# A float32 transformer layer on one core: the down projection turned from feature-major to token-major

## The reference

```python
def rmsnorm(x, g):
    y = x * rsqrt(mean(x * x, axis=-1, keepdims=True) + EPS)
    return y * g

def swiglu_ffn(h, w_gu, w_down):
    g, u = split(h @ w_gu, 2, axis=-1)
    return (silu(g) * u) @ w_down

h = x + gla_mixer(rmsnorm(x, norm_mix_g), ...)
h = h + swiglu_ffn(rmsnorm(h, norm_ffn_g), w_gu, w_down)   # w_down: 2816 x 1024
out = rmsnorm(h, final_norm_g)
```

## Time and profile before

| | us |
|---|---|
| median of 3 runs (lowest, highest) | 2302.48 (2296.62, 2304.03) |
| the profiled execution, its own time | 2303.43 |
| its span, first to last instruction | 2301.7 |
| PE busy | 2182.6 (95%) |
| POOL, DVE, ACT busy | 1614.2, 1338.3, 829.6 |
| mean granted TensorE clock | 0.978 of full |

### The profile page before, as it was taken

One profiled execution on the slowest core, in us unless ns is written; L12 is line 12 of the kernel. 1 busy time (PEld: TensorE's weight loads), 2 busy tenths in 40 slices (PEclk: granted clock), 3 DMA queues, 4 the chain that ended last, 5 costly groups with the idle time before them and its releaser, 6 DMA issues.

```text
span 2301.7 us, 28014 instructions
## 1 busy us (share of the span) xinstructions
PE 2182.6 (95%) x10040; PEld 1808.1 (79%) x10040; DVE 1338.3 (58%) x1765; ACT 829.6 (36%) x1430; POOL 1614.2 (70%) x1300
## 2 busy tenths in 40 slices
PE   6999999899989999789999998999999999999975
PEld 5888788778877888578888886888888788888864
DVE  5345544554555443376666664757575756578756
ACT  3224333333343332343434342444444322222313
POOL 5555675566556665668888885988888877776744
PEclk8999999999999999989999999999999999999988
DMA  4322354335433656563434359444343777667761
GB/s 130 104 82 74 110 170 132 110 111 172 139 110 99 201 158 217 181 233 137 173 129 177 128 180 358 154 149 160 142 164 138 297 262 295 261 244 261 291 256 73
DMA packets 233929, 400.56 MB, mean 174 GB/s; under 512 B 16864, under 2 KB 176608, under 8 KB 224832
## 3 DMA queue, kind: packets, MB, share of 16 engines
q1 hardware_dynamic: 199488, 357.82, 44.0%
q10 hardware_dynamic: 34304, 40.97, 5.3%
HBM read 271.85 MB, written 126.88 MB: 173 GB/s over the span
## 4 chain that ended last, share of the span: by engine, by line
PE 82%; DVE 6%; ACT 4%; DMA 4%; POOL 2%; issue 1%; SPq 0%; ACTq 0%; DVEq 0%; POOLq 0%
PE ps L651 26%; PE ps L653 25%; PE ps L652 25%; PE ps L681 1%; PE ps L765 1%; DVE xs L1368 1%; ACT junk L974 1%; DMA xop<-x_stage 1%; DVE lc L1396 1%; POOL ring_lo L594 1%; DMA hop<-stage 1%; DMA raw<-in_gla_w_out 1%; DMA xs<-in_x 1%; PE ps L738 1%; PE ps L742 1%
## 5 line engine op out<-in xcount | busy, mean ns | idle before, releaser
L602 POOL TENSOR_TENSOR w_op<-w_raw,w_op 128x512 fp32r<-128x512 f32 x330 | 473.5, 1439 | 160.9 <-ACT w_op L964 157.3
L651 PE MATMUL ps<-x_op,w_op 128*128 128x512 f32 x1232 | 484.3, 393 | 20.4 <-issue 12.0
L652 PE MATMUL ps<-x_op,w_op 128*128 128x512 f32 x1232 | 482.8, 392 | 0.0
L653 PE MATMUL ps<-x_op,w_op 128*128 128x512 f32 x1232 | 482.4, 392 | 0.0
L591 POOL TENSOR_SCALAR ring_hi<-raw 128x512 fp32r<-128x512 f32 x256 | 178.7, 698 | 337.9 <-issue 167.6
L594 POOL TENSOR_TENSOR ring_lo<-raw,ring_hi 128x512 fp32r<-128x512 f32 x256 | 350.2, 1368 | 21.3
L964 ACT ACTIVATE w_op<-w_raw 128x512 fp32r<-128x512 f32 x330 | 206.4, 628 | 365.0 <-PE ps L653 171.7
L651 PEld LDWEIGHTS ps<-x_op,w_op 128*128 128x128 f32 x1232 | 233.4, 189 | 72.3 <-issue 23.8
L653 PEld LDWEIGHTS ps<-x_op,w_op 128*128 128x128 f32 x1232 | 233.4, 189 | 48.8
L652 PEld LDWEIGHTS ps<-x_op,w_op 128*128 128x128 f32 x1232 | 233.6, 190 | 48.4
L651 PE MATMUL ps<-hid,w_op 128*128 128x512 f32 x616 | 242.6, 394 | 16.6 <-DVE acc L1745 16.1
(11 more groups left out here) (185 smaller groups left out, 3938.8 us busy)
## 6 DMA issues: line engine op xcount, KB each, us to landing
hop<-stage SPq DMA_DIRECT2D x154, 512.0 KB, 2.8
hid<-hop SPq DMA_DIRECT2D x70, 1024.0 KB, 9.5
raw<-in_gla_w_in SPq DMA_DIRECT2D x192, 256.0 KB, 3.2
w_raw<-in_ffn_w_gu SPq DMA_DIRECT2D x176, 256.0 KB, 3.9
xop<-x_stage ACTq DMA_DIRECT2D x56, 512.0 KB, 3.6
x_op<-xop SPq DMA_DIRECT2D x56, 512.0 KB, 11.1
w_raw<-in_ffn_w_down SPq DMA_DIRECT2D x88, 256.0 KB, 4.5
raw<-in_gla_w_out SPq DMA_DIRECT2D x64, 256.0 KB, 3.1
```

The lines of the kernel that those rows point to most:

```text
L602: pool.tensor_tensor(shaped(q, w_op[i][:, 1, :]), source(q, i), shaped(q, w_op[i][:, 0, :]).bitcast(F32), ALU.subtract).then_inc(op_ready[ ...
L651: pe.matmul(out, l_hi, r_hi, start=first, stop=False, skip_group_check=more)
L652: pe.matmul(out, l_hi, r_lo, start=False, stop=False, skip_group_check=more)
L653: return pe.matmul(out, l_lo, r_hi, start=False, stop=last, skip_group_check=more)
```

## The change

Only the down projection and what follows it change.

- The operands of the matmul are exchanged: a 128-token block of `hid` is stationary, the weight operand moves over all 512 columns. A lane is now a block of 128 tokens (four in each quarter), and the result is token-major, as the residual and the output are. All transposes go (`turn_final`, `turn_tail`).
- A quad is now one pair with all columns; a slice has one or two quads, and both operand sets are held at once (`w_op` and `w_op2`, `w_t2b`, `w_t3b`).
- Slices 0 to 4 of each half go product by product in the order 0, 1, 4, 3, 2, 5, 6 over all four lanes, with two banks for each lane (`BANK_D`); all eight banks are used. The last slice goes lane by lane.
- `hid` has 7 slots, not 9: slot `i` is filled again when product `i` of all four lanes of the slice before is done.
- The residual is added on DVE, SBUF to SBUF, in slices 1 and 3 of each half (`add_ht`, 128 x 1024 each). Product 0, which goes into four quarters, is kept in `p1_sum` up to slice 3 (lanes 0 and 1) or 4 (lanes 2 and 3), then added to three quarters (`spread_p1`), and from there on added three times from the bank.
- The final norm works on `acc` in place: token block by token block in the last slice and (for the rest of half 0) in the first slice of half 1. SP's queue gets the stores of half 0, and the loads of `ht`.

```diff
-        hid = [... for n in range(9)]
+        hid = [sb(f"hid{n}", MIX + 8192 * n, [P, 2, 2, T], F32R) for n in range(7)]
+        BANK_D = (0, 1, 0, 1, 0, 1, 0)
+        IN_TURN, BY_BANK = (0, 1, 2, 3, 4, 5, 6), (0, 1, 4, 3, 2, 5, 6)
+        SUMMED_TO = (3, 3, 4, 4)
+        HT_PARTS = (1, 3)
+        HT_AT = {1: 0, 2: 1, 5: 2, 6: 3}
...
@@ sync @@
             def load_hid(n, i):
+                if n == 0:
+                    sp.wait_ge(prod[i // 2], U_QUADS)
+                else:
+                    sp.wait_ge(prod[i], slices[n]["lane0"])
...
                 if n == 0:
                     for m in range(7):
                         store_hid(end, m)
+                        if m in (2, 4):
+                            load_quad(slices[1]["quads"][m // 2 - 1])
+                    sp.dma_start(g_fin[:, :], ...).then_inc(fin_loaded, 16)
+                    for slot in range(4):
+                        sp.wait_ge(stage_stored[slot], 16 * ((7 * NP * NS - slot + 3) // 4))
...
@@ tensor @@
+            def lane_product(n, l, i):
+                pairs = slices[n]["pairs"]
+                lane_free(n, l, i)
+                tok = slice(l * P, (l + 1) * P)
+                for j in range(pairs):
+                    w = (w_op, w_op2)[j][i]
+                    ins = three(ps[:, lane_bank(n, l, i), :], hid[i][:, j, 0, tok], hid[i][:, j, 1, tok], w[:, 0, :],
+                                w[:, 1, :], j == 0 and i < 3, j == pairs - 1, i > 2)
+                ins.then_inc(prod[i], 1)
+            for n, part in enumerate(slices):
+                if part["part"] == LAST_SLICE:
+                    steps = [(l, i) for l in range(4) for i in IN_TURN]
                 else:
+                    steps = [(l, i) for i in BY_BANK for l in range(4)]
...
@@ scalar: op_split @@
-                if q > 0:
-                    act.wait_ge(prod[i], lanes_end[q - 1])
+                if second(q) and slice_of[q][0] == 0:
+                    if i > 0:
+                        act.wait_ge(prod[3 if i <= 2 else 4], U_QUADS)
+                elif q > 0:
+                    act.wait_ge(prod[i], lanes_before(q))
...
+                elif q == U_QUADS - 1:
+                    for at, (i, j) in enumerate(made_in(0)):
+                        op_split(U_QUADS + j, i)
+                        if at in (4, 8, 11):
+                            hidden_hi(pair, (4, 8, 11).index(at))
...
+                if before["part"] == LAST_SLICE:
+                    for j in range(3):
+                        for number in range(4):
+                            square_of(0, j, number)
+                            if number == 0 and j > 0:
+                                root_of(0, j - 1)
...
@@ vector: gather @@
+                if i == 0 and part > SUMMED_TO[l]:
+                    for out_half, th in ((0, 1), (1, 1), (1, 0)):
+                        dst = place(n, l, out_half, th)
+                        ins = dve.tensor_tensor(dst, dst, bank, ALU.add)
+                    ins.then_inc(p1_kept, 1)
+                    return
...
+                            elif B == 0:
+                                if (l, i) == (1, 2):
+                                    variance_fin(0, 0)
+                                elif (l, i) == (1, 3):
+                                    root_fin(0, 0)
+                                elif (l, i) == (1, 4):
+                                    scale_fin(0, 0, 0)
+                                elif (l, i) == (2, 0):
+                                    scale_fin(0, 1, 0)
...
```

More of the change, by code:

```diff
@@ L647, in _, with weigh @@
+            def weigh(j, out_half, squares):
+                pool.wait_ge(squared, SQUARES["fin", 1, j] + squares)
+                cols = slice(out_half * HALF, (out_half + 1) * HALF)
+                tile = acc[1][1][j]
+                pool.tensor_tensor(tile[:, cols], tile[:, cols], g_fin[:, cols], ALU.mult).then_inc(tail_weighed, 1)
+            for j in range(4):
+                weigh(j, 1, 1)
+                weigh(j, 0, 3)
         @block.tensor
@@ L1732, in _ @@
                 sum_3(pair)
-            def place(q, column, out_half, token_half):
-                return acc[d_quads[q - U_QUADS]["B"]][:, column + 4 * out_half, token_half, :]
-            def gather(q, lane, column, product, bank, dst, done, n):
-                dve.wait_ge(prod[product], lane + 1)
-                from_bank = ps[:, 3 * (lane % 2) + bank, :]
-                if n == 0 and d_quads[q - U_QUADS]["part"] == FIRST_SLICE:
-                    ins = dve.tensor_copy(dst, from_bank)
-                else:
-                    ins = dve.tensor_tensor(dst, dst, from_bank, ALU.add)
-                ins.then_inc(done, 1)
@@ L1763, in _, with place @@
-            summed = 0
-            for q in range(U_QUADS, QUADS):
-                d = d_quads[q - U_QUADS]
-                tile = final_tile(q)
-                final = q == QUADS - 1
-                ending = d["part"] == LAST_SLICE and not final
-                def between(i):
-                    if final:
-                        for number in TAIL_AFTER[i]:
-                            tail_add(number)
-                    if q == U_QUADS:
+            def place(n, l, out_half, th):
+                return acc[slices[n]["B"]][th][l][:, out_half * HALF:(out_half + 1) * HALF]
@@ L1784, in between @@
                             sum_4(pair)
                             hidden_lo(pair, 6)
-                    if tile is not None and i == 2:
-                        dve.wait_ge(ht_loaded[tile % 2], 16 * (tile // 2 + 1))
-                        dve.wait_ge(fin_turned, tile + 1)
-                        for half in range(2):
-                            part = ht[tile % 2][:, half * HALF:(half + 1) * HALF]
-                            dve.tensor_tensor(part, part, ps[:, 6 + half, :], ALU.add).then_inc(fin_added, 1)
```

627 lines of the change are left out of this document (310 added, 317 removed).

## The result

| | kernel before | changed kernel |
|---|---|---|
| median of 4 runs | 2302.55 us (2296.62 to 2304.03) | 2280.65 us (2280.23 to 2281.34) |
| ratio | | 0.9905, 95% interval 0.9892 to 0.9917 |
| span of the profiled execution | 2301.7 | 2278.5 |
| first matmul on `hid` starts | 1824.70 | 1826.37 |
| last one starts | 2275.74 | 2268.62 |

The account below looks back on a forecast made before the run. PE, busy 95% of the span, was taken as the bound: last matmul at 2243.4 plus tail 10.1 gave 2253.5; stalls of 4, 3, 4.5 and 1.5 gave span 2266.5, so median 2267 us, range 2254 to 2286.

Parts of the forecast that it names:

- Pace and count: Down projection on PE: still 1848 matmuls at 0.2266 us, 418.7 us in all, with no transposes.
- Tail: Behind the last matmul: only lane 3's last quarter and two last stores, 10.1 us (9 to 13).
- The `y_all` block: Eight `y_all` loads ahead of raw weights in SP's queue: removing them saves 13.07 us and 2.4 of slow clock.
- Place 1: Start of down: late gathers behind ACT's hidden pieces, and a late `hid` load for slice 1; 4 us (0 to 10).
- Place 2: Slice 3 of each half: residual adds and spreads make DVE late for slice 4; 1.5 us each (0 to 4).
- Place 3: Last slices: 0.3 us lost in each of eight lanes, about 2 in lane 2 of half 0; 4.5 us (2 to 9).
- Place 4: First slice of half 1: DVE's wait for lane 3's squares covered unless Newton steps eat the slack; 1.5 us (0 to 5).
- POOL: Each slice: 14 splits and 8 sums take 30 of 38.1 us, so POOL is not the bound; no loss forecast.
- The slow clock behind a wait: PE at 1.2 GHz for part of the time: 2.4 us counted in the kernel before, nothing for new gaps.
- Rival A: Whole stage: all stalls covered except 0.3 us in each of eight lanes, giving 2257 us; chance 0.13.
- rival B: DVE becomes the bound in places through slow SBUF-to-SBUF operations: 36 us of stalls, giving 2290 us; chance 0.18.
- Rival C: SP's in-order queue holds up loads: four places at 13.1 us each, giving 2320 us, slower than before; chance 0.04.

Follow-up runs that it names:

- the first edit: Changed kernel with ACT's hidden pieces of the last pair made two places earlier: 2278.36 us, ratio 0.9900.
- three edits: On the changed kernel, each alone: ACT's hidden pieces earlier, 2278.36 us; root ahead of square in half 0's last slice, 2279.78; residual tile 2 added behind product 6, 2282.86.
- the two that relieved POOL: On the changed kernel: raw weights loaded by quarter as freed (alone 2276.57 us), and POOL's two last sums moved directly ahead of product 5's splits (not run alone).
- five edits: Changed kernel with quarter loads, earlier ACT pieces, root ahead of square, POOL's last sums later, and residual tile 2 added behind product 6: 2265.16 us, ratio 0.9839.

## Why the prediction was right, and where it was off

The sign, the range and the mechanism held; the sum of the stalls was mis-sized. Span 2278.5 against 2266.5 forecast, step by step:

- **Pace and count: right.** 1848 matmuls at 0.2266, no change by exchanging operands, no transposes.
- **Start of the stage: 1.7 of the 12.0.** It began at 1826.37 instead of 1824.70, and between 1820.53 and 1825.56 in the experiments. This is scatter of the stages before.
- **Tail: right in sum, by two errors that cancel.** 10.1 forecast, 9.65 measured. Up to the last store it took 5.2 instead of 4.6, with two gathers and two squares behind the last matmul where I had one of each; from the store to the end 4.5 instead of 5.5. (By the earlier trace rows the time between landing and the end was 7.5 - 5.3 = 2.2 before, not 1.5.) Its first and last rows:

```profile
2268.80 1.27 DVE L1803 TENSOR_TENSOR acc<-acc,ps 128x512 f32<-128x512 f32 x2
...
2272.85 1.28 DVE L1394 SCALAR_TENSOR_TENSOR acc<-acc,rstd,g_fin 128x1024 f32<-128x1024 f32 x1
2274.03 0.34 ACTq L1333 DMA_DIRECT2D out<-acc  x1
```

- **The `y_all` block: right.** 13.07 + 2.4 forecast; the run with that edit alone gave 16.9 by the medians and 15.5 in its profile.
- **Place 1, 4 forecast, 5.2 found.** The first half was right in kind: ACT's piece came behind splits and DVE waited for it, but ahead of the very first gathers of slice 0, for ACT itself had waited 9.64 us for POOL's last sums. DVE's and ACT's timelines:

```profile
1836.62 1.84 DVE L1370 TENSOR_TENSOR stage<-s,stage 128x512 fp32r<-128x512 f32 x1 [6.11 <-ACT stage L983]
...
1840.05 2.47 DVE L1801 COPY p_sum<-ps 128x512 f32<-128x512 f32 x4
```

```profile
1834.19 0.63 ACT L983 ACTIVATE w_op<-w_raw 128x512 fp32r<-128x512 f32 x1 [9.64 <-POOL w_raw L640]
```

  The `hid` load behind it was covered in this profile. In four others it came out with this delay in place, 0.2 to 1.8 us (1.17 in the changed kernel run again, near 1864 as I had said) and in the five without the delay it was 1.5 to 2.1.
- **Place 2, 3 forecast, 8.4 found** (3.64 + 4.74). The place and the engine were right, and so, nearly, was DVE's work: ahead of the last gathers of slice 3 stand three residual adds and six spreads, 3 x 3.0 + 6 x 1.5 = 18.0 by my allowance, and they took 17.2 in half 0 (with a wait of 2.75 for the tile's load, which stood in SP's queue behind loads of `hid`) and 18.3 in half 1, with one add of 5.62. PE idled 1.83 and 2.93, where I had 2 for this allowance and took 1.5. The slow clock behind the two waits added 1.8 each, and this is most of what was missing. Both rows are of DVE in the changed kernel:

```profile
1964.15 1.98 DVE L1822 TENSOR_TENSOR acc<-acc,ht 128x1024 f32<-128x1024 f32 x1 [2.75 <-DMA ht<-hres]
...
2159.82 5.62 DVE L1822 TENSOR_TENSOR acc<-acc,ht 128x1024 f32<-128x1024 f32 x1
```

  The same sum, taken in the nine profiles that have the adds in this order, tells whether there is a gap: up to 15.3 us there was none (seven places), from 15.5 to 18.4 PE idled the sum minus 15.35 (ten places, to within 0.03). One does not fit: 2.69 at a sum of 16.7, with a wait of 4.0 for the tile's load. With the last slice of half 1 by product the sum was 14.9 in both halves, without POOL's last sum 14.3 and 15.5, so both fall under this account.

- **Place 3, 4.5 forecast, 7.2 found.** 0.3 in a lane was exact (0.31). For lane 2 of half 0 I gave 2, and it was 5.66, of it 1.9 behind the wait, in the slow clock: the root stood behind lane 1's square as forecast, and ACT loaded a function table first, so that DVE waited 2.31 us for it, before two Newton steps of 0.60 and 1.14 beside POOL. By the run with the root first about 1.1 of the wait hung on that order (2.52 to 1.44):

```profile
2025.33 1.28 ACT L988 ACT_TABLE_LOAD   x1
```

- **Place 4, 1.5 forecast, nothing found.**
- **POOL, nothing forecast, 2.2 found** (8.6 + 1.0 in the second profile of the same kernel). This is the step that failed: "POOL needs 14 splits and 8 sums in a slice, 22 x 1.35 = 30 of 38.1 us [...]: neither is the bound". I compared sums of busy time. The 22 operations took 30 to 33 us, and I left out that both raw buffers are now held to the end of the loop, which adds 4 to 6 us of idle time to it (33 to 39 in all), and that the lane-by-lane slice wants product 2 at 2.7 us, where a slice by product wants it at 21.8. What the first edit closed ahead of it came back here. In the first profile the term is small; what it was worth shows only in the runs: 14.8 us without POOL's last sums.
- **Two readings of rows were off.** 1.27 for a small operation beside POOL is the mean of the earlier trace rows, not its most; and the 1.5 of the tail, above.
- **The slow clock behind a wait, nothing forecast, 7.3 of the above.** In the four longer gaps, idle times of 11.4 us made PE 18.7 us late. I had counted this for the kernel before (2.4) and left it out for every new gap, and it is over half of the 12.0 us. So the largest term missing from the sum was one that my rows already showed.

The time lies near the upper end of the forecast's own range (2258 to 2282), so the range held by its width, not by the sum. Rival A is out. Of rival B the mechanism was at work in places only: adds with both inputs in SBUF took 1.35 us in the mean for 512 columns and 1.85 for 1024, while the gathers from PSUM stayed at 0.685. By the Trainium skill, page SBUF — State Buffer, section on the two separate sides, the loser of the two engines waits for the whole of the other's operation. The longest case of this profile, the add of 5.62 us from 2159.82, goes beyond one operation; POOL's timeline beside it is

```profile
2156.84 7.51 POOL L622 TENSOR_TENSOR w_op<-w_raw,w_op 128x512 fp32r<-128x512 f32 x6
```

Six splits back to back, until 2164.35, and the add ended at 2165.44, 1.1 later, where the shortest takes 1.22 in all: DVE seems to have waited for the whole row of splits. It is no single case. Over all profiles of the changed kernel and its edits eleven adds took 5.3 to 6.6 us, at this same place, and each ended 1.07 to 1.09 us behind POOL's last split of a row of five or six. In nineteen other cases an add fell into such a row, took 1.4 to 2.4, and in most of them POOL's six splits took 8.5 to 9.4 us instead of 7.5. What decides between the two was not tested, nor was POOL taken away from beside this add alone. Rival C is out: the longest wait for a load that reached PE was DVE's for a residual tile, 2.75 us here and 4.01 in the changed kernel run again.

DVE's groups from 1825 to 2280:

```profile
L1816 DVE TENSOR_TENSOR acc<-acc,p_sum 128x512 f32<-128x512 f32 x24 | 31.4, 1348 | 0.4
L1822 DVE TENSOR_TENSOR acc<-acc,ht 128x1024 f32<-128x1024 f32 x16 | 29.6, 1847 | 4.6 <-DMA ht<-hres 4.2
```

## What to carry to other kernels

An engine that prepares operands is not ruled out as a bound by its busy share: write down its loop, with the reload that can only start when its last operation frees a buffer, and compare the time at which it has each operand ready with the moment at which the consumer wants it, which a new order of the consumer can move by some 20 us. Price a new gap with the slow clock behind it, not by its idle time alone. When closing single gaps brings nothing, look where the next one opened: here three edits were worth nothing apart and 14 us together with the two that relieved POOL. And before a large rewrite is credited, take its smallest part alone: moving eight loads was worth 17 of the 22 us.

## What the runs showed of the hardware that was not expected

- Behind idle pieces of TensorE of 1.83, 2.87, 2.93 and 3.79 us seven or eight matmuls ran 0.43 us apart (granted clock 0.57 in 1841 to 1845), 1.8 to 1.9 us more each. It is not sure to happen: in the second profile of the same kernel a wait of 2.89 us made PE only 3.13 late, and with the root first one of 3.07 made it 3.32 late.
- The same add of two SBUF tiles of 1024 columns took between 1.22 and 5.62 us (6.60 with five edits). The long ones began inside a row of POOL's operations without a break and ended 1.1 us behind the whole row; others that began inside such a row took 1.4 to 2.4.
- Ahead of ACT's first root behind the squares stood a table load of 1.28 us (2025.33), in the middle of a chain in which DVE waited. It is the last load in the profile: the later roots, behind squares too, had none.
- Executions of one kernel with equal times can have their gaps in other places: 3.64 us at slice 4 and 1.51 at slice 5 in one, none and 8.60 in the other.
